# First two projection units in step with the normalisation, k-tile by k-tile, in a one-core diffusion-backbone kernel

## The reference

```python
# layer 0 (even)
h = rmsnorm(x, norm_mix_g[0]) * (1 + scale1) + shift1
p = h @ w_in                                  # the "in" stage: 28 blocks of 128 output columns
y = concat(delta_net(p...), short_conv(p...)) @ w_out
x = x + gate1 * y
# layer 1 (odd): y = multiscale_pool(h, w_pool); x = x + gate1 * y
# both layers
h = rmsnorm(x, norm_ffn_g) * (1 + scale2) + shift2
u = dwconv3(h @ w_gate, conv)                 # 22 blocks of 128 columns
x = x + gate2 * ((silu(u) * (h @ w_up)) @ w_down)
```

## Time and profile before

| what | value |
|---|---|
| median of 3 runs | 1600.87 us (1600.68 to 1606.43) |
| profiled execution | 1601.7 us |
| its span | 1599.9 us |
| PE busy | 1427.5 us (89%) |
| PE weight loads busy | 1385.3 us (87%) |
| DVE busy | 1008.9 us (63%) |
| POOL busy | 658.2 us (41%) |
| ACT busy | 390.3 us (24%) |

### The profile page before, as it was taken

The page is one execution under the profiler, slowest core; times in us unless marked ns, Lnnn a source line. Parts: engine busy times, 40 slices in busy tenths (PEclk is TensorE's granted clock), DMA queues, the critical chain, the costliest instruction groups (busy, mean ns, idle before and its releaser), DMA issues.

```text
span 1599.9 us, 24831 instructions
## 1 busy us (share of the span) xinstructions
PE 1427.5 (89%) x9517; PEld 1385.3 (87%) x9517; DVE 1008.9 (63%) x1376; ACT 390.3 (24%) x703; POOL 658.2 (41%) x400
## 2 busy tenths in 40 slices
PE   3799999744897979999999999986999999999995
PEld 1599989633896969999999999975999999999995
DVE  4788658795356457887787887645565145415554
ACT  4711141342444161100110011156333011101122
POOL 0255435200131525566555655420445445445452
PEclk9899999876998989999999999998999999999998
DMA  9033434210001223444334434210232221222222
GB/s 370 30 105 105 161 102 127 73 66 0 1 2 46 99 69 128 176 146 157 122 114 141 149 131 139 72 59 8 92 112 85 79 77 68 71 86 66 77 69 77
DMA packets 42913, 154.23 MB, mean 96 GB/s; under 512 B 4592, under 2 KB 5744, under 8 KB 41968
## 3 DMA queue, kind: packets, MB, share of 16 engines
q1 hardware_dynamic: 42864, 153.61, 28.1%
HBM read 150.45 MB, written 3.15 MB: 96 GB/s over the span
## 4 chain that ended last, share of the span: by engine, by line
PE 76%; DVE 13%; ACT 4%; issue 3%; DMA 2%; ACTq 0%; POOL 0%; DVEq 0%; SPq 0%; POOLq 0%
PE ps L588 67%; PE ps L856 1%; DVE junk L1329 1%; DVE blocks L1517 1%; DVE ada_raw L1329 1%; DVE blocks L1520 1%; ACT work L1057 1%; DMA ada_raw<-in_w_rows 1%; ACT work L925 1%; PE ps L600 1%; DMA x<-in_x 1%; PE ps L668 1%; PE ps L734 1%; PE ps L810 1%; PE ps L808 1%
## 5 line engine op out<-in xcount | busy, mean ns | idle before, releaser
L520 POOL TENSOR_SCALAR whi<-raw 128x1024 fp32r<-128x1024 f32 (+1 forms) x172 | 191.0, 1111 | 842.1 <-PE ps L588 605.1
L588 PE MATMUL ps<-hhi,whi 128*128 128x320 f32 x1984 | 458.7, 312 | 32.5 <-DVE hlo L1313 30.9
L588 PE MATMUL ps<-hlo,whi 128*128 128x320 f32 x1984 | 455.1, 311 | 0.0
L588 PE MATMUL ps<-hhi,wlo 128*128 128x320 f32 x1984 | 454.6, 311 | 0.0
L523 POOL TENSOR_TENSOR wlo<-raw,whi 128x1024 fp32r<-128x1024 f32 (+1 forms) x172 | 436.4, 2537 | 14.3
L588 PEld LDWEIGHTS ps<-hhi,whi 128*128 128x128 f32 x1984 | 334.3, 190 | 38.4 <-issue 27.3
L588 PEld LDWEIGHTS ps<-hlo,whi 128*128 128x128 f32 x1984 | 335.2, 190 | 0.0
L588 PEld LDWEIGHTS ps<-hhi,wlo 128*128 128x128 f32 x1984 | 334.8, 190 | 0.0
L588 PE MATMUL ps<-hidhi,whi 128*128 128x320 f32 x704 | 161.2, 310 | 4.8 <-POOL wlo L523 3.4
L588 PE MATMUL ps<-hidlo,whi 128*128 128x320 f32 x704 | 160.9, 310 | 0.0
L588 PE MATMUL ps<-hidhi,wlo 128*128 128x320 f32 x704 | 160.6, 309 | 0.0
(11 more groups left out here) (190 smaller groups left out, 1271.8 us busy)
## 6 DMA issues: line engine op xcount, KB each, us to landing
raw<-in_w_gu SPq DMA_DIRECT2D x88, 512.0 KB, 3.3
ada_raw<-in_w_rows SPq DMA_DIRECT2D x80, 512.0 KB, 3.5
raw<-in_w_in SPq DMA_DIRECT2D x28, 512.0 KB, 3.3
raw<-in_w_dn SPq DMA_DIRECT2D x32, 448.0 KB, 3.3
ada_first<-in_w_ada SPq DMA_DIRECT2D x4, 2048.0 KB, 22.2
raw<-in_w_dn SPq DMA_DIRECT2D x16, 512.0 KB, 3.6
raw<-in_w_out SPq DMA_DIRECT2D x8, 512.0 KB, 3.9
x<-in_x SPq DMA_DIRECT2D x1, 2560.0 KB, 11.0
```

Source lines behind the costliest of these rows:

```text
L520: nc.gpsimd.tensor_scalar(whi[s][:, 0:n], raw[s][:, 0:n], 1.0, 0.0, ALU.mult, ALU.add).then_inc(s_whi, 1)
L588: last = nc.tensor.matmul(pair[pr][:, b], wt[s][:, cs], act[:, k, b * HALF:(b + 1) * HALF], start=(j == 0 and q == 0), stop=(j == len(tile ...
```

## The change

Three things. In the three stages, PE's first two units run in step (`first_units`): product k of unit 0, then product k-1 of unit 1, with the wait for k-tile k ahead of unit 0's product; PE waits for unit 1's split and pair B only at k = 1. The third unit's weights are split into a third pair, `whi[2]`/`wlo[2]`, without the guard, directly behind the first two splits (`second_pair`; in layer 1 behind a wait for `s_mix >= 8`, since the third pair lies over `rows_tok`, which the mixer's last matmuls read). The fourth unit uses pair 1 again, with the guard. The Fori loops then begin at their third iteration (i = 2), and the wait per k-tile is gone from their bodies. No arithmetic is changed, and the number of matmuls, splits and loads is the same.

```diff
--- before.py
+++ after.py
@@ -231,6 +231,8 @@
         w_mix = nc.alloc_sbuf_tensor_at("w_mix", [P, 4, 2, 2 * P], F32, offset=band_at + 4 * W * 4)
         rows_tok = nc.alloc_sbuf_tensor_at("rows_tok", [P, 2, len(MIX_TILES), 2 * P], F32,
                                            offset=band_at + 4 * W * 4 + 2 * SLOT * 4)
+        whi.append(nc.alloc_sbuf_tensor_at("whi2", [P, SLOT], F32R, offset=o4 - 8 * SLOT))
+        wlo.append(nc.alloc_sbuf_tensor_at("wlo2", [P, SLOT], F32R, offset=o4 - 4 * SLOT))
         h_mix = nc.alloc_sbuf_tensor_at("h_mix", [P, KD, W], F32, offset=off_h)
         cond_rows = nc.alloc_sbuf_tensor_at("cond_rows", [P, 2, D], F32, offset=o4)
         assert band_at + 4 * W * 4 + 2 * SLOT * 4 + 2 * len(MIX_TILES) * 2 * P * 4 <= o4
@@ -395,7 +397,7 @@
 
         def ada_split(n):
 
-            return (whi + more[0:2])[n % 4], (wlo + more[2:4])[n % 4]
+            return (whi[0:2] + more[0:2])[n % 4], (wlo[0:2] + more[2:4])[n % 4]
 
         block = ctx.enter_context(nc.Block())
 
@@ -512,15 +514,16 @@
 
         @block.gpsimd
         def _(pool):
-            def split(u, half_u, s, n=SLOT, guard=True):
+            def split(u, half_u, s, n=SLOT, guard=True, to=None):
+                to = s if to is None else to
                 pool.wait_ge(s_raw[s], half_u * 16 + 16)
                 if guard:
                     pool.wait_ge(s_unit, u - 1)
                 pool.sem_inc(s_go, 1)
-                nc.gpsimd.tensor_scalar(whi[s][:, 0:n], raw[s][:, 0:n], 1.0, 0.0,
+                nc.gpsimd.tensor_scalar(whi[to][:, 0:n], raw[s][:, 0:n], 1.0, 0.0,
                                         ALU.mult, ALU.add).then_inc(s_whi, 1)
                 pool.wait_ge(s_whi, u + 1)
-                nc.gpsimd.tensor_tensor(wlo[s][:, 0:n], raw[s][:, 0:n], whi[s][:, 0:n].bitcast(F32),
+                nc.gpsimd.tensor_tensor(wlo[to][:, 0:n], raw[s][:, 0:n], whi[to][:, 0:n].bitcast(F32),
                                         ALU.subtract).then_inc(s_split, 1)
 
             def split_pairs(u, n_pairs, n=SLOT, first=0):
@@ -528,10 +531,15 @@
                     for s in range(2):
                         split(i * 2 + (u + s), i + u // 2, s, n)
 
+            def second_pair(u):
+                split(u + 2, u // 2 + 1, 0, guard=False, to=2)
+                split(u + 3, u // 2 + 1, 1)
+
             pool.wait_ge(s_ada_pe, ADA_FIRST)
             for s in range(2):
                 split(s, 0, s, guard=False)
-            split_pairs(0, 14, first=1)
+            second_pair(0)
+            split_pairs(0, 14, first=2)
 
             pool.wait_ge(s_gd, 4)
             pool.wait_ge(s_row_sums, ADA_IN)
@@ -565,7 +573,14 @@
 
                     pool.wait_ge(s_a, 24)
                 for g, nf in enumerate(GROUPS):
-                    split_pairs(SEG["up", layer, g]["u"], nf)
+                    u = SEG["up", layer, g]["u"]
+                    if g == 0:
+                        for s in range(2):
+                            split(u + s, u // 2, s)
+                        if layer == 1:
+                            pool.wait_ge(s_mix, 8)
+                        second_pair(u)
+                    split_pairs(u, nf, first=(2 if g == 0 else 0))
                     split_pairs(SEG["down", layer, g]["u"], 4, nf * P)
 
             pool.wait_ge(s_rstd, 5)
@@ -576,20 +591,44 @@
 
         @block.tensor
         def _(pe):
+            def product(pr, s, tile, act_hi, act_lo, k, first, final):
+
+                cs = slice(tile * P, tile * P + P)
+                for q, (wt, act) in enumerate(((whi, act_hi), (whi, act_lo), (wlo, act_hi))):
+                    for b in range(2):
+                        last = nc.tensor.matmul(pair[pr][:, b], wt[s][:, cs], act[:, k, b * HALF:(b + 1) * HALF],
+                                                start=(first and q == 0), stop=(final and q == 2))
+                return last
+
             def products(pr, s, tiles, hi, lo, ks, wait_k=None):
 
                 last = None
                 for j, (tile, k) in enumerate(zip(tiles, ks)):
                     if wait_k is not None:
                         wait_k(j)
-                    cs = slice(tile * P, tile * P + P)
-                    for q, (wt, act) in enumerate(((whi, hi), (whi, lo), (wlo, hi))):
-                        for b in range(2):
-                            last = nc.tensor.matmul(pair[pr][:, b], wt[s][:, cs],
-                                                    act[:, k, b * HALF:(b + 1) * HALF],
-                                                    start=(j == 0 and q == 0),
-                                                    stop=(j == len(tiles) - 1 and q == 2))
+                    last = product(pr, s, tile, hi, lo, k, j == 0, j == len(tiles) - 1)
                 return last
+
+            def first_units(u, a, b, wait_k):
+
+                pe.wait_ge(s_split, u + 1)
+                pe.wait_ge(s_ev["A"], a)
+                for k in range(KD + 1):
+                    if k < KD:
+                        wait_k(k)
+                        last = product("A", 0, k, hhi, hlo, k, k == 0, k == KD - 1)
+                        if k == KD - 1:
+                            last.then_inc(s_unit, 1)
+                    if k == 1:
+                        pe.wait_ge(s_split, u + 2)
+                        pe.wait_ge(s_ev["B"], b)
+                    if k:
+                        last = product("B", 1, k - 1, hhi, hlo, k - 1, k == 1, k == KD)
+                last.then_inc(s_unit, 1)
+                for s in range(2):
+                    pe.wait_ge(s_split, u + 3 + s)
+                    pe.wait_ge(s_ev["AB"[s]], (a, b)[s] + 1)
+                    products("AB"[s], (2, 1)[s], range(KD), hhi, hlo, range(KD)).then_inc(s_unit, 1)
 
             def ada(n):
 
@@ -637,9 +676,10 @@
                 pe.wait_ge(s_ev["AB"[s]], half_u + PRIMED)
                 products("AB"[s], s, range(KD), hhi, hlo, range(KD), wait_k).then_inc(s_unit, 1)
 
-            with pe.Fori(0, NQKV // 2) as i:
+            first_units(0, PRIMED, PRIMED, lambda k: pe.wait_ge(s_h, PRIMED + k + 1))
+            with pe.Fori(2, NQKV // 2) as i:
                 for s in range(2):
-                    in_unit(i * 2 + s, i, s, (lambda j: pe.wait_ge(s_h, PRIMED + j + 1)) if s == 0 else None)
+                    in_unit(i * 2 + s, i, s)
 
             pe.wait_ge(s_mod, 1)
             for k in range(KD):
@@ -883,12 +923,13 @@
                 for g, nf in enumerate(GROUPS):
                     b = SEG["up", layer, g]
                     hr = 8 if layer == 0 else 16
-                    with pe.Fori(0, nf) as i:
+                    if g == 0:
+                        first_units(b["u"], b["A"], b["B"], lambda k: pe.wait_ge(s_h, PRIMED + hr + k + 1))
+                    with pe.Fori(2 if g == 0 else 0, nf) as i:
                         for s in range(2):
                             pe.wait_ge(s_split, i * 2 + (b["u"] + s + 1))
                             pe.wait_ge(s_ev["AB"[s]], i + b["AB"[s]])
-                            wait_k = (lambda j: pe.wait_ge(s_h, PRIMED + hr + j + 1)) if s == 0 and g == 0 else None
-                            products("AB"[s], s, range(KD), hhi, hlo, range(KD), wait_k).then_inc(s_unit, 1)
+                            products("AB"[s], s, range(KD), hhi, hlo, range(KD)).then_inc(s_unit, 1)
                     f = b["f"]
                     accumulate(("down", layer, g), nf, hidhi, hidlo, lambda j: pe.wait_ge(s_hid, f + j + 1))
                 norm_sums(2 if layer == 0 else 4)
```

## The result

The changed kernel takes 1606.4 us, median of 21 runs (1604.4 to 1610.16), against 1604.2 us for the kernel before in 21 runs beside them (1600.58 to 1606.67). The ratio is 1.0019, 95% interval 1.0011 to 1.0026: 3.0 us slower (1.8 to 4.2), where 2.9 us faster was forecast. 1606.4 lies outside the range as well.

A forecast was written before the change was run, and what follows sets the result against it. PE's matmuls were taken as the bound, with first-unit holes to fill. In stage 0.0, layer 0 -2.3 and layer 1 -0.6 gave -2.9 us: 1598.0 on the 1600.87 median, 8-in-10 range 1593 to 1602.5.

The forecast's parts named there:

- the ceilings: First unit of three stages: filling PE's holes gains at most 3.0 (in stage), 3.5 (layer 0), 3.7 (layer 1), 10.2 us together.
- the collision eats the in stage's ceiling: In stage: the third pair's early split delays DVE's k-tiles, costing +3.0 against the 3.0 us gain; net 0.
- Layer 0's share: Layer 0: the early split delays DVE's first normalisation and every k-tile; cost +0.9 us (0 to 1.0).
- In the in stage no such stall: In stage, behind the first two units: copy, convolution, SiLU and copy of B end at about 6.5 of 7.04 us.
- a lag of 3 to 6 us is worked off in a few pairs while PE goes on: Pairs behind the first units: DVE, busy 67 of 77.7, 80 of 98.5 and 59 of 98.4 us, catches up.
- rival (b): First pairs of each stage: DVE becomes the bound, deciding from 0.5 us stall per pair; about 1605 us, chance 12%.
- the late first unit: Behind the two units, now ending 1.76 us apart: PE waits 0.3 us in layer 0, 1.25 in layer 1.
- I take 0.3: Layer 0: two row sums may make the next pair's multiplication late, 21.5 us against 21.1 wanted; 0.3 us (0 to 1.5).
- Cost +1.85: Layer 1, before the norm: the early split holds up DVE's addition of squares and what follows; +1.85 us (0 to 2.4).
- the pairs behind layer 1's first unit: Layer 1: PE waits 0.5 us for ACT's copy, 0.0 to 1.2 more for the multiplication; 1.25 us (0 to 2.5).
- L: Post-measurement theory, not forecast: unit 0 ends about 5 us later in step, so DVE and ACT start late and cannot catch up.
- C: Post-measurement theory, not forecast: the third pair's early split holds up what makes the k-tiles and the norm.

The follow-up runs named there:

- e3: Changed kernel, but the third pair's split waits for each stage's last k-tile; 1600.36 us, 0.9976 of the kernel before.
- the square: Four kernels as ratios to the kernel before: in step or trailing, split early or late; the changed kernel, e3, e10, e4: 1.0019, 0.9976, 0.9980, 0.9947.
- e7: Kernel before, plus eight small DVE writes ahead of the in stage's first convolution; 1607.55 us, 1.0019 of the kernel before.
- e4: As e3, but unit 1 trails unit 0 instead of alternating with it; 1595.11 us, 0.9947 of the kernel before.
- e9: Changed kernel, with one of two row sums behind layer 0's first pair moved further on; 1610.06 us, 1.0046 of the kernel before.
- e1: Changed kernel with the in stage back in the old order, both feed-forward stages as changed; 1601.22 us, 0.9981 of the kernel before.
- e6: Changed kernel's third pair and early split, but all of unit 0 and then all of unit 1; 1611.18 us, 1.0038 of the kernel before.
- e10: e4 without its two POOL waits, so the third pair's split is early again; 1600.23 us, 0.9980 of the kernel before.
- e8: e4's trailing order without a third pair, the third unit's split waiting for unit 0; 1610.8 us, 1.0035 of the kernel before.
- e11: The same kernel as e4, run on another occasion; 1594.45 us, 0.9949 of the kernel before.
- e2: Changed kernel with only the in stage in step, both feed-forward stages in the old order; 1605.96 us, 1.0014 of the kernel before.

## Why the prediction was wrong

**Right: the ceilings.** 16.35 us were worked out for the 16 products in layer 0 and 16.25 measured; in layer 1 16.3 (20.0 - 3.7) and 15.8, which with a wait of 0.6 us behind them make the 16.45 of the table. In the in stage it was 16.7 without a collision (19.7 - 3.0), and e3 shows 16.91. PE was full at the low clock, and the k-tiles did not bind at the end.

**Right: that the collision eats the in stage's ceiling.** Net 0 forecast, +0.3 measured, by the hlo of 2.97 us and a PE gap of 2.4 us (3 forecast). Layer 0's share was 0.9 forecast and 0.6 measured. The Trainium skill, page "SBUF — State Buffer", section "Who interferes with whom", which the prediction weighed, is agreed with once more, and further than I used it: it lists tensor_scalar too among the operations that can contend with GpSimd, when their operands meet certain conditions. In this trace the convolution's first step L1383 takes 0.55 us alone and 1.41 us when it starts with a whi, as the rows below show. I had counted only on the two-input operations.

**Wrong, the step that turned the sign: "In the in stage no such stall", and behind it "a lag of 3 to 6 us is worked off in a few pairs while PE goes on".** This was rival (b), in the stage where I had excluded it. The sum held 1.55 us for the late first unit (0.3 in layer 0, 1.25 in layer 1, nothing in the in stage). The parts show 1.8 in the in stage, 2.3 in layer 0 and 2.0 in layer 1, 6.1 us together, and the square prices it at 4.3 to 6.9. With 6.1 in place of 1.55 the forecast of -2.9 would have been +1.7. I read DVE's busy 67 of 77.7 us as 10.7 us of room. There is none: the idle time sits in waits that belong to the same cycle. POOL's split starts when PE ends a unit, DVE's convolution when ACT has copied that unit, and the two fall on each other in the same way in every pair. Before, the first convolution step began 0.58 us behind whi and lost part of it. DVE and POOL of the kernel after, in order of time:

```profile
83.42 0.55 DVE L1383 TENSOR_SCALAR work<-work,cols 128x640 f32<-128x640 f32 x1 [5.42 <-ACT work L1027]
...
119.83 1.41 DVE L1383 TENSOR_SCALAR work<-work,cols 128x640 f32<-128x640 f32 x1 [1.49 <-ACT work L1027]
```

```profile
119.83 1.06 POOL L523 TENSOR_SCALAR whi<-raw 128x1024 fp32r<-128x1024 f32 x1 [3.35 <-PE ps L599]
```

And the kernel before, DVE in an earlier pair, with the same place in its cycle (each of its pairs looks so):

```profile
99.85 0.80 DVE L1342 TENSOR_SCALAR work<-work,cols 128x640 f32<-128x640 f32 x1 [1.50 <-ACT work L986]
```

With the convolution released exactly as whi starts, its first step takes 1.41 us for 0.80, and the chain DVE-ACT-DVE of a pair, 14.08 us long before (steps of 6.96 and 7.12 us in turn between convolutions), becomes 14.63 (6.92 and 7.71), over PE's 14.08. In the pairs ahead of that the same 0.6 us falls on the next step, L1386 beside wlo (3.85 us at 105.79 for 3.02), and the chain is 14.6 us long already. So the lateness is not worked off: it grows until PE's two units take 7.12 and 7.51 us, a loss of 0.55 us in each pair (0.3 of it shows as the wait on the copy). The prediction asked for a stall of 0.5 us per pair as the point from which (b) decides; it was 0.55. e7 shows it without any of the change's other parts. Its price in the ten units is 1.8 us after and 2.2 in e7.

**Mis-sized: "I take 0.3" for the second multiplication in layer 0.** It was 2.3. The mechanism was the one named (two row sums behind the first pair), and the figure was not worked out. In the trace after the two sums took 4.6 and 3.2 us where 2.3 is usual, their first and last halves having splits beside them, and the next convolution's first step 2.67:

```profile
602.85 0.82 DVE L1704 TENSOR_TENSOR work<-work,ps 128x640 f32<-128x640 f32 x1 [0.88 <-ACT work L1276]
...
606.20 3.41 DVE L1370 SCALAR_TENSOR_TENSOR junk<-ada_raw,cond_rows 128x1024 bf16<-128x1024 f32 x1
...
614.00 2.67 DVE L1383 TENSOR_SCALAR work<-work,cols 128x640 f32<-128x640 f32 x1
...
619.65 0.82 DVE L1704 TENSOR_TENSOR work<-work,ps 128x640 f32<-128x640 f32 x1 [0.88 <-ACT work L1276]
```

The multiplication ends at 620.47, 23.3 us after the two units (PE's third unit starts at 597.15), where 21.5 had been put down as the worst and 21.1 was wanted. The trailing order removes it by starting this work earlier (e4, 7.04), and e9 by taking one sum away. That DVE is still late three pairs further on, in e9, is the failed step again, in layer 0.

**Mis-sized: layer 1's norm, "Cost +1.85".** The addition lost 1.86 us, as forecast, but the part became 3.1 to 3.2 us longer (2.7 in e1, 2.8 in e6, 2.5 in e10, 0.1 in e3). 0.5 us of the rest is a term that I had not thought of. PE, idle 4.43 us instead of 2.57 before its eight norm sums, took 4.64 us for them instead of 4.11, at the low clock. This pair of numbers is the same in all traces: 4.63 to 4.64 us behind 4.43 idle in six, 4.11 to 4.19 us behind 2.57 or 2.58 idle in seven. The stretch around the sums, first of the kernel before, then after (the clock stands third from the end):

```profile
1099.00:1104.00 5.00, 3.58 (x8) 1.91 (x6) 0.34 (x2) 3.58 (x5) 0.00 (x0) 0.68 0.00 0
```

```profile
1109.00:1114.00 5.00, 4.23 (x8) 2.12 (x7) 0.46 (x2) 2.95 (x4) 0.00 (x0) 0.50 0.24 96
```

The remaining 0.1 to 0.8 us lie in the mixer's rows ahead of the sums (first to last matmul 34.22 us before; 34.97 and 35.06 in the two traces of the changed kernel, 34.65 in e6, but also in e8, which has no early split) and are not assigned.

**Right in kind, too small: the pairs behind layer 1's first unit.** 1.25 forecast (0.5 and up to 1.2 more); 2.0 measured: 0.6 for ACT's copy behind the table load, as named, and 1.4 for the multiplication. PE in order of time after, at the first of the two:

```profile
1136.72 0.46 PE L599 MATMUL ps<-hhi,wlo 128*128 128x320 f32 x2
1137.66 0.53 PE L599 MATMUL ps<-hhi,whi 128*128 128x320 f32 x2 [0.48 <-ACT work L1273]
```

So the forecast -2.9 was 0.0 - 2.3 - 0.6, and the parts measured after are +2.1 in the in stage, -0.6 in layer 0 and +1.0 in layer 1, with +1.3 to +1.8 between the in stage and the out stage that I had no term for.

**What stays open.** "816-864" is longer by 0.2 to 1.0 us in all kernels but before, e1, e6 and e11, and "1200-1344" by 0.6 to 1.5 us in those ones and e11, except e4, where it is 2.1 us shorter; both lie behind the in stage's first twelve units, mostly in kernels whose chain or start was changed there, and no cause was shown. The sum of parts, without the three laid aside, agrees with the measured difference within 1.7 us for eight of the twelve timed kernels, the change itself among them; in e1, e2, e8 and e10 it is 2.0 to 3.8 us too high. e1 and e2 not adding up to the change (-0.8 against +3.0) is of this size. Nothing of the verdict on L and C rests on it: each is shown in its own part of the trace and by a ratio whose interval excludes 1.

## What to carry to other kernels

Filling PE's holes with a second unit is worth its ceiling only if the engines behind it keep their lead on PE's next units: let the second one trail, so that the first ends when it did (a lead of 2.7 us was enough here, 0.7 was not). Idle time of a follower engine in a steady loop is not room to catch up until the waits in it are shown to shrink when it starts late; compare its chain per period (14.08 us here) with the bound engine's (14.08). And when a split is moved, give it a place behind the last operation on whose result PE is waiting, since the VectorE instruction beside a GpSimd one can lose most of the other's length (here up to 2.15 of 2.80 us).

## What the runs showed of the hardware

I had not expected three things. Two engines that meet in each period can lock into the worse of two patterns and stay there: 14.63 us a pair in the in stage after, 14.6 in e8's layer 1, for 14.08 us of PE work, with the same instructions and only their start shifted by 5 us. VectorE's single-input step L1383 is held by GpSimd as well, 0.55 us alone, 0.80 when it starts 0.58 us into whi, 1.41 when it starts with it, and 2.67 in layer 0's second pair, beside a wlo. And behind a PE idle time of 4.43 us instead of 2.57 the eight matmuls of the norm sums were granted 0.50, the 1.2 GHz level, in the stretch around them instead of 0.68 (4.64 us busy against 4.11).
